# Weighting and summing the two experts' rows by diagonal matmuls, and the final norm in one VectorE pass

## The reference

```python
def rmsnorm(x, g):
    xf = x.astype(jnp.float32)
    y = xf * lax.rsqrt(jnp.mean(xf * xf, axis=-1, keepdims=True) + RMS_EPS)
    return (y * g.astype(jnp.float32)).astype(x.dtype)
...
    x = x + gt2 * hier_moe(h2, w_rg, b_rg, w_re, b_re, w1, w3, w2)
...
    y_prompt = rmsnorm(xp, normf_g)
    y_sample = rmsnorm(xs, normf_g)
```

## Time and profile before

| what | value |
|---|---|
| median of 3 runs | 1290.59 us (1285.94, 1290.59, 1291.39) |
| the profiled execution, device time | 1285.97 us |
| its span, first to last instruction | 1284.1 us |
| PE, DVE, ACT, POOL busy | 92%, 47%, 32%, 15% |
| mean granted clock of PE | 0.963 of full |
| last matmul ends | about 1234.8 us |
| first and last gather issued | 1239.61 and 1251.00 us |
| SP's last output DMA issued | 1279.10 us |

### The profile page before, as it was taken

One profiled execution on the slowest core, in us unless ns is written; L12 is line 12 of the kernel. 1 busy time (PEld: TensorE's weight loads), 2 busy tenths in 40 slices (PEclk: granted clock), 3 DMA queues, 4 the chain that ended last, 5 costly groups with the idle time before them and its releaser, 6 DMA issues.

```text
span 1284.1 us, 23541 instructions
## 1 busy us (share of the span) xinstructions
PE 1177.6 (92%) x9563; PEld 1066.2 (83%) x9563; DVE 608.9 (47%) x1127; ACT 411.0 (32%) x634; POOL 190.4 (15%) x282
## 2 busy tenths in 40 slices
PE   3789999999999999999899999995999999999940
PEld 2588888988899999886599999995989898989830
DVE  1544565645555644532644444666243433334236
ACT  5323242323242232321444444330223132322224
POOL 0153354443341000000000000003000000000024
PEclk9899999999999999999899999996999999999975
DMA  9999868878566697568888873944999999999433
GB/s 308 338 378 338 300 237 276 292 264 283 202 222 223 223 378 261 174 223 312 324 290 295 295 254 93 318 156 180 333 393 347 338 339 336 347 335 336 166 120 101
DMA packets 189292, 350.75 MB, mean 273 GB/s; under 512 B 11363, under 2 KB 110203, under 8 KB 187126
## 3 DMA queue, kind: packets, MB, share of 16 engines
q1 hardware_dynamic: 180694, 326.75, 72.8%
q0 software_dynamic: 6304, 14.50, 3.3%
q10 hardware_dynamic: 2224, 8.52, 2.0%
HBM read 320.17 MB, written 117.65 MB: 341 GB/s over the span
## 4 chain that ended last, share of the span: by engine, by line
PE 85%; DVE 6%; DMA 4%; issue 2%; ACT 1%; POOL 1%; SPq 0%; POOLq 0%; DVEq 0%; ACTq 0%
PE psum L819 43%; PE psum L1157 18%; PE psum L1174 7%; PE psum L895 3%; PE psum L881 2%; PE psum L870 2%; PE psum L770 2%; PE psum L861 2%; PE psum L917 1%; DMA kvr<-in_cache_v_dram 1%; DMA adar<-in_w_ada_dram 1%; PE psum L1132 1%; PE psum L944 1%; PE psum L777 1%; DVE ya L1999 1%
## 5 line engine op out<-in xcount | busy, mean ns | idle before, releaser
L819 PE MATMUL psum<-hHi,whi 128*128 128x272 f32 x1216 | 359.8, 296 | 5.8 <-DVE hLo L1487 3.0
L819 PE MATMUL psum<-hLo,whi 128*128 128x272 f32 x1216 | 352.4, 290 | 0.0
L819 PE MATMUL psum<-hHi,wlo 128*128 128x272 f32 x1216 | 350.7, 288 | 0.0
L819 PEld LDWEIGHTS psum<-hHi,whi 128*128 128x128 f32 x1216 | 230.1, 189 | 23.7 <-issue 18.7
L1157 PEld LDWEIGHTS psum<-xgT,e 128*128 128x128 f32 x2048 | 234.1, 194 | 3.2 <-issue 1.5
L1157 PE MATMUL psum<-xgT,e 128*128 128x96 f32 x2048 | 233.9, 277 | 1.3 <-DVE xgT L1954 1.3
L819 PEld LDWEIGHTS psum<-hHi,wlo 128*128 128x128 f32 x1216 | 230.4, 189 | 0.0
L819 PEld LDWEIGHTS psum<-hLo,whi 128*128 128x128 f32 x1216 | 229.6, 189 | 0.0
L1439 DVE TENSOR_TENSOR wlo<-wraw,whi 128x1024 fp32r<-128x1024 f32 x100 | 131.4, 1317 | 68.4 <-ACT whi L1218 68.1
L1961 DVE TENSOR_TENSOR e2Lo<-e,e2Hi 128x2048 fp32r<-128x2048 f32 x32 | 71.9, 2289 | 143.5 <-ACT e2Hi L1383 143.5
L1218 ACT ACTIVATE whi<-wraw 128x1024 fp32r<-128x1024 f32 x100 | 104.7, 1051 | 27.1 <-PE psum L819 21.4
(11 more groups left out here) (319 smaller groups left out, 1808.7 us busy)
## 6 DMA issues: line engine op xcount, KB each, us to landing
e<-in_w_dram SPq DMA_DIRECT2D x48, 2048.0 KB, 10.1
wraw<-in_w_in_dram SPq DMA_DIRECT2D x76, 512.0 KB, 5.4
out_dram<-in_cache_k_dram SPq DMA_DIRECT2D x32, 1022.0 KB, 8.9
out_dram<-in_cache_v_dram SPq DMA_DIRECT2D x32, 1022.0 KB, 7.8
adar<-in_w_ada_dram SPq DMA_DIRECT2D x36, 512.0 KB, 6.2
kvr<-in_cache_k_dram SPq DMA_DIRECT2D x8, 2048.0 KB, 9.2
kvr<-in_cache_v_dram SPq DMA_DIRECT2D x8, 2048.0 KB, 8.6
out_dram<-in_cache_k_dram SPq DMA_DIRECT2D x8, 1016.0 KB, 7.4
```

What stands on the lines that cost most here:

```text
L819: mm = pe.matmul(psum[:, t, 0:HALF], w[:, slot, k, :], x[:, k, cols], start=(k == 0 and n == 0), stop=(k == k_n - 1 and n == 2))
```

## The change

- `weigh`, a new tile of 10 matrices of 128x128 (over the first 5 KB of `toks`, whose tables 0 and 1 are no longer read by then), is made by DVE ahead of the expert loop: the identity with its rows multiplied by `cw`, one for each tile and choice.
- After the expert loop PE waits for each tile's gathered rows and computes diag(cw0) ya + diag(cw1) yb2 in four f32 matmuls: two halves of 512 columns, two sources added up in PSUM. The five tiles use banks 0 to 7 in turn (two each, tile 4 those of tile 0).
- DVE reads the sum out of PSUM and multiplies it by the gate, then adds the residual. The two weighting steps on ACT and DVE go (L1393, L1992).
- The final norm is one DVE instruction, (x2 * rstd) * weight, for what L1411 on ACT and L2105 on POOL did. POOL ends with the gathers.
- ACT takes a root of unused columns after the expert loop; the table of the root is loaded with it. Per tile it keeps the square and the root.
- DVE's order of a turn is: gate of tile tt, mean of tt-1, residual of tt, reciprocal and norm of tt-1.
- The semaphores x2_half, op_half and ya_done go, with their waits; f_gate, y_pe and weigh_done are new.

```diff
@@ -246,6 +246,7 @@
+    weigh = Region(toks_at)("weigh", [P, 2, TILES + 1, P])
@@ -1020,7 +1021,6 @@
-                    pe.wait_ge(x2_half, f)
@@ -1082,7 +1082,6 @@
-            pe.wait_ge(x2_half, KC)
@@ -1174,6 +1173,20 @@
                                 mm = pe.matmul(psum[0:TS, 6 + n, :], x[:, fc, :], w[:, fc, :],
                                                start=(part == 0 and fc == 0), stop=(part == 2 and fc == FC - 1))
                         mm.then_inc(ye_pe, 1)
+
+
+            for tt in range(TILES + 1):
+                n = P if tt < TILES else NS
+                pe.wait_ge(yg_in[tt], 32)
+                if tt == 0:
+                    pe.wait_ge(weigh_done, 2 * (TILES + 1))
+                if tt >= 4:
+                    pe.wait_ge(f_gate, tt - 3)
+                for c in range(2):
+                    for r_, src in enumerate((ya, yb2)):
+                        mm = pe.matmul(psum[0:n, 2 * (tt % 4) + c, :], weigh[0:n, r_, tt, 0:n],
+                                       src[0:n, tt, 512 * c:512 * c + 512], start=(r_ == 0), stop=(r_ == 1))
+                mm.then_inc(y_pe, 1)
         @block.scalar
@@ -1342,7 +1355,6 @@
-                act.wait_ge(x2_half, f + 1)
@@ -1387,28 +1399,17 @@
                     act.wait_ge(ye_ev0, 2 * jp + (q + 2))
                     act.wait_ge(ye_ev1, 2 * jp + (q + 2))
                     act.dma_start(y_rows[bass.ds((2 * jp + q) * TS, TS), :], yev[:, q, :]).then_inc(ye_out[q], 16)
-            def first_choice(tt):
-                n = P if tt < TILES else NS
-                act.wait_ge(yg_in[tt], 32)
-                act.activation(ya[0:n, tt], ya[0:n, tt], ACT.Copy, scale=cw[0:n, 0, tt:tt + 1]).then_inc(ya_done, 1)
-
-            first_choice(0)
-            for tt in range(TILES + 2):
-                if tt:
-                    a = tt - 1
-                    n = P if a < TILES else NS
-                    act.wait_ge(f_mix, a + 1)
-                    if a:
-                        act.wait_ge(f_sq, a)
-                    act.activation(junk3[0:n, :], x2[0:n, a, :], ACT.Square,
-                                   accum_out=stat[0:n, a:a + 1]).then_inc(f_sq, 1)
-                if tt < TILES:
-                    first_choice(tt + 1)
-                if tt:
-                    act.wait_ge(ms_done, a + 3)
-                    act.activation(rstd[0:n, a:a + 1], stat[0:n, a:a + 1], ACT.Sqrt).then_inc(sqrt_done, 1)
-                    act.wait_ge(rec_done, a + 2)
-                    act.activation(x2[0:n, a, :], x2[0:n, a, :], ACT.Copy, scale=rstd[0:n, a:a + 1]).then_inc(xn_done, 1)
+            act.wait_ge(sqrt_done, 3)
+            act.activation(rstd[:, TILES + 1:8], stat[:, TILES + 1:8], ACT.Sqrt).then_inc(sqrt_done, 1)
+            for a in range(TILES + 1):
+                n = P if a < TILES else NS
+                act.wait_ge(f_mix, a + 1)
+                if a:
+                    act.wait_ge(f_sq, a)
+                act.activation(junk3[0:n, :], x2[0:n, a, :], ACT.Square,
+                               accum_out=stat[0:n, a:a + 1]).then_inc(f_sq, 1)
+                act.wait_ge(ms_done, a + 3)
+                act.activation(rstd[0:n, a:a + 1], stat[0:n, a:a + 1], ACT.Sqrt).then_inc(sqrt_done, 1)
         @block.vector
@@ -1745,7 +1746,7 @@
                     own(dve.memset(sqp[:, :, :], 1.0))
                 cols = slice(P * f, P * f + P)
                 dve.tensor_tensor(x2[:, 0:TILES, cols], psum[:, 2 + f % 2, :].rearrange("p (a n) -> p a n", n=P),
-                                  x2[:, 0:TILES, cols], ALU.add).then_inc(x2_half, 1)
+                                  x2[:, 0:TILES, cols], ALU.add)
                 dve.tensor_tensor(x2[0:NS, TILES, cols], psum[0:NS, 4, 0:P], x2[0:NS, TILES, cols], ALU.add)\
                    .then_inc(x2_done, 1)
@@ -1753,7 +1754,6 @@
-                dve.wait_ge(x2_half, f + 1)
@@ -1773,7 +1773,6 @@
-                        ins.then_inc(op_half, 1)
@@ -1787,7 +1786,6 @@
-                dve.wait_ge(op_half, f + 1)
@@ -1953,6 +1951,10 @@
             for n in range(2):
                 dve.tensor_copy(xgT[:, 0, 4 * n:4 * n + 4, :], psum[:, 4 * n:4 * n + 4, 0:TS]).then_inc(xgT_ev, 1)
             dve.wait_ge(bcT_ev, 6)
+            for r_ in range(2):
+                for tt in range(TILES + 1):
+                    dve.tensor_scalar(weigh[:, r_, tt, :], ident[:, :], cw[:, r_, tt:tt + 1], None, ALU.mult)\
+                       .then_inc(weigh_done, 1)
             with dve.Fori(0, pairs) as jp:
                 for q in range(2):
                     for n in range(2):
@@ -1981,27 +1983,33 @@
             dve.wait_ge(late_in, 128)
-            for tt in range(TILES + 2):
-                a = tt - 1
+
+            def normalised(a):
                 m = P if a < TILES else NS
-                if tt <= TILES:
-                    n = P if tt < TILES else NS
-                    tab_ = tokt if tt < TILES else toks
-                    dve.wait_ge(yg_in[tt], 32)
-                    dve.wait_ge(ya_done, tt + 1)
-                    own(dve.scalar_tensor_tensor(ya[0:n, tt], yb2[0:n, tt], cw[0:n, 1, tt:tt + 1], ya[0:n, tt],
-                                                 ALU.mult, ALU.add))
+                dve.wait_ge(sqrt_done, a + 5)
+                own(dve.reciprocal(rstd[0:m, a:a + 1], rstd[0:m, a:a + 1]))
+                dve.scalar_tensor_tensor(x2[0:m, a, :], x2[0:m, a, :], rstd[0:m, a:a + 1], tokt[0:m, 0, :],
+                                         ALU.mult, ALU.mult).then_inc(f_y, 1)
+
+            def mean_square(a):
+                m = P if a < TILES else NS
+                dve.wait_ge(f_sq, a + 1)
+                dve.tensor_scalar(stat[0:m, a:a + 1], stat[0:m, a:a + 1], 1.0 / D, EPS, ALU.mult, ALU.add)\
+                   .then_inc(ms_done, 1)
+
+            for tt in range(TILES + 1):
+                n = P if tt < TILES else NS
+                dve.wait_ge(y_pe, tt + 1)
+                dve.tensor_tensor(ya[0:n, tt], psum[0:n, 2 * (tt % 4):2 * (tt % 4) + 2, :].rearrange("p b n -> p (b n)"),
+                                  (tokt if tt < TILES else toks)[0:n, 2, :], ALU.mult).then_inc(f_gate, 1)
                 if tt:
-                    dve.wait_ge(f_sq, a + 1)
-                    dve.tensor_scalar(stat[0:m, a:a + 1], stat[0:m, a:a + 1], 1.0 / D, EPS, ALU.mult, ALU.add)\
-                       .then_inc(ms_done, 1)
-                if tt <= TILES:
-                    own(dve.tensor_tensor(ya[0:n, tt], ya[0:n, tt], tab_[0:n, 2, :], ALU.mult))
+                    mean_square(tt - 1)
+                dve.wait_ge(f_gate, tt + 1)
+                dve.tensor_tensor(x2[0:n, tt, :], x2[0:n, tt, :], ya[0:n, tt], ALU.add).then_inc(f_mix, 1)
                 if tt:
-                    dve.wait_ge(sqrt_done, a + 4)
-                    dve.reciprocal(rstd[0:m, a:a + 1], rstd[0:m, a:a + 1]).then_inc(rec_done, 1)
-                if tt <= TILES:
-                    dve.tensor_tensor(x2[0:n, tt, :], x2[0:n, tt, :], ya[0:n, tt], ALU.add).then_inc(f_mix, 1)
+                    normalised(tt - 1)
+            mean_square(TILES)
+            normalised(TILES)
         @block.gpsimd
@@ -2098,11 +2106,7 @@
-            pool.wait_ge(late_in, 128)
-            for tt in range(TILES + 1):
-                n = P if tt < TILES else NS
-                pool.wait_ge(xn_done, TILES + 2 + tt)
-                pool.tensor_tensor(x2[0:n, tt, :], x2[0:n, tt, :], tokt[0:n, 0, :], ALU.mult).then_inc(f_y, 1)
+
```

More of the change, by code:

```diff
@@ L514, in _build @@
         opT_pe = sem("opT_pe")
-        x2_half = sem("x2_half")
         x2_done = sem("x2_done")
-        op_half = sem("op_half")
         bc_done = sem("bc_done")
@@ L556, in _build @@
         ye_out = [sem("ye_out0"), sem("ye_out1")]
-        ya_done = sem("ya_done")
         yg_in = [sem(f"yg_in{k}") for k in range(TILES + 1)]
         f_mix = sem("f_mix")
+        f_gate = sem("f_gate")
+        y_pe = sem("y_pe")
+        weigh_done = sem("weigh_done")
         f_sq = sem("f_sq")
```

## The result

The kernel after took 1278.28 us in the median (1274.87 to 1280.50, eight runs), the kernel before, timed with it, 1287.76 us (1284.03 to 1291.66, eight runs). The ratio is 0.9927, with a 95% interval of 0.9911 to 0.9943: 9.4 us less by the ratio, between 7.3 and 11.5. The profiled execution took 1278.32 us, its span is 1276.5 us.

What follows compares the result with a forecast made beforehand. The tail after PE's last matmul was taken as bound by VectorE, stretched by GpSimd, its end by GpSimd's drain. Last rows 4.8 us earlier plus 2.7 at the end gave 7.5 off 1290.59: 1283.1 us, 8-in-10 range 1277.5 to 1289.

Steps and rivals of the forecast that it cites:

- Gathers and weights: Tail gathers unchanged; ten diagonal VectorE products at the expert loop's head take 2.3 us, hidden, adding 0.
- rival B: At the expert loop's head, diagonal products delay the last scatter, at most 1.9 us at the first expert; 1285.0; chance 0.13.
- Dropped semaphores: Removing x2_half and op_half, where PE is full, gains nothing; a few tens of ns each, hidden.
- Matmuls: Weighted sum on PE after the expert loop: 3.44 us a tile at full clock, 6.8 at half; clock rises after 4.6.
- Rival C: In the tail PE never leaves the half clock level, making the kernel slower: 1295.7 us; chance 0.05.
- VectorE's turn: One tile's gate, mean square, add, reciprocal and norm pass take 4.18 us, bounding the tail from tile 1 on.
- No stretched gate: With nothing but gathers left on GpSimd, no VectorE operation in the tail is stretched to 3.1 us; gate 1.23.
- rival D: The tail's gate product stays slow because of output transfers beside it, not GpSimd: 1288.8 us; chance 0.07.
- Last tile: From the last tile's gate to its last rows 6.1 us; rows ready at 1274.3 against 1279.07, 4.8 us earlier.
- The end: Without GpSimd's late drain, the span ends 2.35 us after the last rows instead of 5.07, gaining 2.7 us.
- Table load: The root table's 1.28 us load moves into ScalarE's idle time before 1246; nothing is added to the path.
- The sum: Whole kernel: last rows at 1274.3 plus 2.35 end the span at 1276.6, 7.5 us under 1284.1; named time 1283.1.

Runs made afterwards that it cites:

- e9: Kernel after with tile 0 weighted on ScalarE and VectorE, and idle PE matmuls before tile 1 and at the routing stage; 1277.12 us, ratio to before 0.9921.
- e1: Kernel before with only the final norm made one VectorE pass, weighting left on ScalarE and VectorE; 1283.79 us, ratio to before 0.9944.
- e7: Kernel after without the early load of the root's table; 1286.22 us in one run, 40.53 us from the yev copy to the end.
- e3: Kernel after plus a one-column GpSimd memset that waits for the last tile's norm; 1283.66 us, ratio to before 0.9952.
- e2: Kernel after with the norm put back on ScalarE and GpSimd, weighting still on PE; 1286.21 us, ratio to before 0.9962.
- e4: Kernel after plus twelve idle PE matmuls between the expert loop and the first gathered tile; 1278.78 us, ratio to before 0.9902.

## Why the prediction was right, step by step

*Gathers and weights: right.* The first gather comes 4.79 us after the yev copy, 4.78 before. The ten products took 2.04 us (2.3 named), and the slack of 0.42 us at the first expert was kept; rival B did not occur in this kernel. The delay that the rule in the Trainium skill (SBUF — State Buffer, "SBUF: two separate sides") would have allowed did not show: 8.98 and 8.82 us against 8.72 for the scatter with the products right on its issue. At most 0.3 us could be such a delay, and the 9.46 of e9 stays open. That the full DMA queue is the reason was argued and is not shown. *Dropped semaphores:* no run takes them apart from the rest, and they were put at nothing. The first scatter, which comes behind the stretch that they stood in, starts anywhere from 879.97 to 888.40 us in the twelve profiles, with the semaphores or without, so this stays open.

*Matmuls: right.* A record is 0.43 us at the upper level, 0.85 at the lower; the clock rose after 5.0 us (4.6 named, 2.9 and 6.3 as bounds). Tile 1's gate came 9.6 us after the first rows, 9.5 forecast. Rival C is out. Its "gap of 1.3 us was enough" is what the trace before shows (the granted clock is 0.99 in 895 to 896 and 0.50 from 896 on), but e9's gap of 1.67 us lost nothing, so the length of a gap doesn't settle it.

*VectorE's turn: the mis-sized term.* I added whole lengths and small waits to 4.18 us; it was 3.79. The five lengths in the trace add up to 4.02, and the rows overlap by 0.23 in all: after each of the three long operations the next row starts 0.08 us before it ends. The other 0.16 are waits that were added and didn't show. Over three turns that is 1.2 us too many.

*No stretched gate: right*, by 1.20 to 1.23 us on every tile in the trace after and in e1, with the output transfers still beside it; rival D is out.

*Last tile: 6.1 forecast, 5.62 measured*, from its gate at 1268.16 to the end of the pass at 1273.78. The rows overlap there in the same way; I haven't divided the 0.5 us up.

*The end: 2.35 forecast, 2.72 measured.* SP needed 2.5 us from its last issue to its drain, where the earlier trace rows had 2.1. That GpSimd's drain was the long one, and would be gone, was right.

*Table load: the step that put nothing on the path was right* for this kernel (e7).

*The sum.* From the yev copy on, the forecast was 1276.6 - 1234.83 = 41.8 us, measured 40.5: 1.3 too many, the sum of the terms above (1.2 and 0.5 too many, 0.4 too few). The span of 1276.5 meets the forecast of 1276.6 partly by luck, since the loop ended 1.16 us later than before in that profile. The time named, 1283.1, started from the median of three runs shown, 1290.59; over eight runs the median before is 1287.76, which is 2.8 of the 4.8 us by which 1278.28 lies below it, and the larger gain is the rest. The chance of "faster" rested on the line at 0.5% being only just passed; the measured ratio passes it with its whole interval.

## What to carry to other kernels

Look at who drains last: where the trace has an engine whose drain outlasts the last output by microseconds, give its last instruction to another engine before tuning the work itself. Where one engine's instruction holds up another's, either of two edits may free it, and the gain comes once, so price the two together and not each by itself. Ask also what the freed engine is given to do: in e1 the passes used up what two shorter gates had saved, and the gain lay in the last tile and the end. And read the turn of a full engine from start to start; lengths added up overstate it.

## What the runs showed of the hardware

- A last GpSimd instruction near the end keeps the kernel open, a small one like a large one: its drain ends 4.8 us behind the end of a memset of 0.10 us (e3) and of a product of 2.33 (before). With SP last it is 2.6 to 2.7 us from the last rows to the end.
- A VectorE product of two SBUF inputs that starts beside a GpSimd product ends 1.07 or 1.08 us after it, 3.1 us long instead of 1.23 (three times in the trace before). With one input in PSUM it takes 1.21 beside the same product (e2).
- ScalarE loads a function's table while the activation that needs it still waits for its input (load at 1264.99, input at 1265.82).
- The row behind a VectorE operation of 1.2 us starts 0.08 us before that ends; in a turn of 3.79 us such overlaps are 0.23.
- After 11 us of idleness PE began at the lower level and was given the upper after 5.0 us of matmuls. Fillers ending 1.02 us (e4) or 1.67 us (e9) before the real work kept it there; behind the matmuls at the head of the loop a wait of 2.71 us (e9) lost it, and so did one of 1.30 us in the trace before.
